# Weight low parts in two half-width GpSimd instructions, and the gated product rounded by ScalarE in the first two blocks

## The reference, cut to what matters

```python
def swiglu(x, w_gate, w_up, w_down):
    return (jax.nn.silu(x @ w_gate) * (x @ w_up)) @ w_down

x = x + 0.5 * swiglu(rms_norm(x, ffn1_norm[l]), ffn1_w_gate[l], ffn1_w_up[l], ffn1_w_down[l])
...      # mixer: indexer-selected sparse attention and multiscale pooling, w_in, w_out
x = x + 0.5 * swiglu(rms_norm(x, ffn2_norm[l]), ffn2_w_gate[l], ffn2_w_up[l], ffn2_w_down[l])
```

## Time and profile before

| | |
|---|---|
| median of 3 runs | 1928.82 us (1926.11 to 1929.69) |
| profiled execution | 1931.76 us, of it span 1930.0 us |
| mean granted TensorE clock | 0.961 |
| PE, PE weight load | 1820.7 us (94%), 1507.3 us (78%) |
| DVE, ACT, POOL | 1132.9 us (59%), 620.0 us (32%), 754.8 us (39%) |

### The profile page before, as it was taken

The page is one execution under the profiler, slowest core; times in us unless marked ns, Lnnn a source line. Parts: engine busy times, 40 slices in busy tenths (PEclk is TensorE's granted clock), DMA queues, the critical chain, the costliest instruction groups (busy, mean ns, idle before and its releaser), DMA issues. The chain is left out here.

```text
span 1930.0 us, 25162 instructions
## 1 busy us (share of the span) xinstructions
PE 1820.7 (94%) x8729; PEld 1507.3 (78%) x8729; DVE 1132.9 (59%) x1648; ACT 620.0 (32%) x1033; POOL 754.8 (39%) x370
## 2 busy tenths in 40 slices
PE   7999999999979999999999999899998699999995
PEld 6887778787756788788887888799887487887874
DVE  4525865867994368354145166565578764364467
ACT  4222112143455332122123133655512442232322
POOL 3543433447660235444444445100033144444434
PEclk9999999999989899999999999999999699999997
DMA  6435543533210245433323333100022133333211
GB/s 200 121 94 156 155 145 89 162 110 93 82 39 22 88 123 182 142 99 96 116 79 105 89 98 98 34 1 2 1 77 77 33 98 113 95 98 98 86 56 44
DMA packets 279689, 178.34 MB, mean 92 GB/s; under 512 B 6264, under 2 KB 258356, under 8 KB 279476
## 3 DMA queue, kind: packets, MB, share of 16 engines
q1 hardware_dynamic: 265348, 149.35, 26.7%
q10 hardware_dynamic: 14256, 27.87, 4.4%
HBM read 175.11 MB, written 2.10 MB: 92 GB/s over the span
## 5 line engine op out<-in xcount | busy, mean ns | idle before, releaser
L604 POOL TENSOR_TENSOR wL<-raw,wH 128x1024 fp32r<-128x1024 f32 (+2 forms) x280 | 681.6, 2440 | 1129.5 <-ACT wH L1126 1128.5
L672 PE MATMUL ps<-actH,wH 128*128 128x512 f32 x1280 | 507.6, 397 | 9.1 <-DVE actL L1878 5.6
L672 PE MATMUL ps<-actL,wH 128*128 128x512 f32 x1280 | 504.0, 394 | 0.0
L672 PE MATMUL ps<-actH,wL 128*128 128x512 f32 x1280 | 503.8, 394 | 0.0
L1126 ACT ACTIVATE wH<-raw 128x1024 fp32r<-128x1024 f32 (+2 forms) x280 | 285.8, 1029 | 452.3 <-PE ps L672 430.6
L672 PEld LDWEIGHTS ps<-actH,wH 128*128 128x128 f32 x1280 | 243.7, 190 | 64.8 <-issue 8.3
L672 PEld LDWEIGHTS ps<-actH,wL 128*128 128x128 f32 x1280 | 243.9, 191 | 51.9
L672 PEld LDWEIGHTS ps<-actL,wH 128*128 128x128 f32 x1280 | 244.1, 191 | 50.1
L672 PE MATMUL ps<-hidH,wH 128*128 128x512 f32 x656 | 261.0, 398 | 17.0 <-DVE hidL L1479 7.8
L672 PE MATMUL ps<-hidL,wH 128*128 128x512 f32 x656 | 259.4, 395 | 0.0
L672 PE MATMUL ps<-hidH,wL 128*128 128x512 f32 x656 | 259.1, 395 | 0.0
(11 more groups left out here) (293 smaller groups left out, 2267.4 us busy)
## 6 DMA issues: line engine op xcount, KB each, us to landing
mod_raw<-in_w_mod ACTq DMA_DIRECT2D x24, 1024.0 KB, 5.1
raw<-in_w_in SPq DMA_DIRECT2D x48, 512.0 KB, 3.7
raw<-in_ffn_w_gate SPq DMA_DIRECT2D x44, 512.0 KB, 3.9
raw<-in_ffn_w_up SPq DMA_DIRECT2D x44, 512.0 KB, 3.8
raw<-in_w_up SPq DMA_DIRECT2D x44, 512.0 KB, 3.8
raw<-in_ffn_w_down SPq DMA_DIRECT2D x32, 512.0 KB, 3.8
raw<-in_w_out SPq DMA_DIRECT2D x16, 512.0 KB, 3.9
raw<-in_w_down SPq DMA_DIRECT2D x16, 512.0 KB, 3.9
```

The lines of the kernel that those rows point to most:

```text
L604: nc.gpsimd.tensor_tensor(wL[:, a:a + w], raw[:, a:a + w], wH[:, a:a + w].bitcast(F32), ALU.subtract).then_inc(lo_ready, 1)
L672: return nc.tensor.matmul(out, a, b, start=first, stop=last)
```

## The change

Two edits. In `lows` the one subtraction of a slab becomes two of half the width, one behind the other, each of which raises `lo_ready`; everything that counts `lo_ready` counts twice as far, so that PE and SP still wait for both halves. In `hidden` DVE no longer rounds `h`: ACT does, in `drain` at odd j, ahead of the split of that slab, on a semaphore `h_ready`, and DVE waits for `h_high` before `hidL`. The counts of links in the loops fall by those that are gone. The feed-forward of the second block and the merge keep their own rounding on DVE.

```diff
         def slab(st, i, j, first=False):
             if not first:
-                sp.wait_ge(lo_ready, i * 4 + (st["base"] + j - 3))
+                sp.wait_ge(lo_ready, (i * 4 + (st["base"] + j - 3)) * 2)
...
                 pool.wait_ge(hi_ready, i * 4 + (st["base"] + j + 1))
-                nc.gpsimd.tensor_tensor(wL[:, a:a + w], raw[:, a:a + w], wH[:, a:a + w].bitcast(F32),
-                                        ALU.subtract).then_inc(lo_ready, 1)
+                for b in (a, a + w // 2):
+                    nc.gpsimd.tensor_tensor(wL[:, b:b + w // 2], raw[:, b:b + w // 2], wH[:, b:b + w // 2].bitcast(F32),
+                                            ALU.subtract).then_inc(lo_ready, 1)
...
                 for j in range(SLOTS):
-                    pe.wait_ge(lo_ready, i * 4 + (st["base"] + j + 1))
+                    pe.wait_ge(lo_ready, (i * 4 + (st["base"] + j + 1)) * 2)
...
                 if j % 2 == 0:
                     act.wait_ge(drained_v, i * 4 + (drain_base[name] + j + 1))
                     nc.scalar.activation(sg[:], g1[:], ACT.Silu).then_inc(silu_ready, 1)
+                else:
+                    f = i * 2 + j // 2
+                    act.wait_ge(h_ready, f + (SILU_BEFORE[name] + 1))
+                    nc.scalar.activation(tile(hidH, f), h[:], ACT.Copy).then_inc(h_high, 1)
...
             dve.wait_ge(silu_ready, f + (SILU_BEFORE[name] + 1))
-            link(V.tensor_tensor(h[:], sg[:], ur[:], ALU.mult))
-            link(V.tensor_scalar(tile(hidH, f), h[:], 1.0, None, ALU.mult))
+            V.tensor_tensor(h[:], sg[:], ur[:], ALU.mult).then_inc(h_ready, 1)
+            dve.wait_ge(h_high, f + (SILU_BEFORE[name] + 1))
             V.tensor_tensor(tile(hidL, f), h[:], tile(hidH, f).bitcast(F32), ALU.subtract).then_inc(hid_ready, 1)
```

More of the change, by code:

```diff
@@ L364, in _build @@
     silu_ready = sem("silu_ready")
+    h_ready, h_high = sem("h_ready"), sem("h_high")
     silu_c_ready = sem("silu_c_ready")
@@ L645, in _ @@
                     pool.wait_ge(q2_rot, 1)
-                    pool.wait_ge(lo_ready, st["base"])
+                    pool.wait_ge(lo_ready, (st["base"]) * 2)
                     for low, half in ((kLA, upper), (kLB, lower)):
@@ L733, in token_tiles @@
             for j in range(SLOTS):
-                pe.wait_ge(lo_ready, st["base"] + j + 1)
+                pe.wait_ge(lo_ready, (st["base"] + j + 1) * 2)
                 for kk in range(2):
@@ L771, in first_slabs @@
                 if k0 == 0:
-                    pe.wait_ge(lo_ready, j + 1)
+                    pe.wait_ge(lo_ready, (j + 1) * 2)
                 for k in range(k0, k1):
@@ L1044, in merge @@
             for j in range(SLOTS):
-                pe.wait_ge(lo_ready, i * 4 + (stage_of["merge"]["base"] + j + 1))
+                pe.wait_ge(lo_ready, (i * 4 + (stage_of["merge"]["base"] + j + 1)) * 2)
                 pe.wait_ge(drained_v, i * 4 + (drain_base["merge"] + j - 3))
@@ L1538, in modded_part @@
             modded(name, n, 0, hid0)
-            chain.loop(1, nf // 2, 2 * ((7 if ctx_too else 3) + 2) + (1 if ctx_too else 0),
+            chain.loop(1, nf // 2, 2 * (7 if ctx_too else 3) + (1 if ctx_too else 0),
                        lambda i: modded(name, n, i, hid0))
@@ L1550, in _ @@
             else:
-                chain.loop(0, nf // 2, 4, lambda i, f0=f0: [hidden("f1_up0", i, q, f0) for q in range(2)])
+                chain.loop(0, nf // 2, 0, lambda i, f0=f0: [hidden("f1_up0", i, q, f0) for q in range(2)])
             if n < 2:
@@ L1737, in _ @@
                             link(V.tensor_scalar(modc[:, 32:40], modc[:, 32:40], 1.0, None, ALU.add))
-                chain.loop(2 if n == 1 else 0, nf // 2, 4,
+                chain.loop(2 if n == 1 else 0, nf // 2, 0,
                            lambda i, n=n, f0=f0: [hidden(f"f2_up{n}", i, q, NF + KT + f0) for q in range(2)])
```

## The result

The changed kernel takes **1908.7 us** (median of 4 runs, 1906.35 to 1912.16); the kernel before took 1927.46 in its runs beside it (1925.87 to 1929.69). The ratio is 0.9903, with a 95% interval of 0.9883 to 0.9923. That is 18.8 us faster. The sign was right, the size was not, and 1911 had been the price of a rival that was given 0.12. One experiment further on (`e11`) has runs at two levels, 45 us apart, and is told with both; one run of `e3` (1940) stands apart from its other three in the same way.

The account below looks back on a forecast made before the run. It took PE, in flight for 94% of the span, to bound the kernel, so only its waits and clock cost time. Terms -1.4+2.1-3.0-2.15+0.4-1.6-0.5 = -6.15 us led to a median of 1922.7, range 1913 to 1931.

Parts of the forecast that it names:

- the size of a hold: DVE beside POOL's low parts: an operation meeting a half waits at most 1.29 us instead of 2.4.
- +0.6 per iteration: Stages where DVE multiplies for the modulation: each iteration grows by 0.6 us, blocked time passing to the products.
- `f1_up1` and `f2_up0`: First and second block's modulated up stages: +2.1 us (-1 to +4) and -2.15 us (-3.8 to +1).
- `f1_up2`'s end: Change to the down stage: wait of 2.12 us becomes 0.3 to 1.0, without clock loss: -3.0 us.
- The rounding on ACT: Ends of f1_up0, f2_up1 and f2_up2: hidL done 3.1 us after the slab, waits of 0.3 and 1.00 removed: -1.4 us.
- the new wait in `f1_down1`: PE waits there for the last modulation products, 2.9 us, and pays the clock again, 1.7.
- Clock: PE at half clock behind waits of some 2.1 us: 1.7 us of work lost each.
- Third block: Its three waits for hidL: no gain, 0 us, since chains of two or more blocked operations gain nothing.
- L1901 at 1.3 and L1902 above 1: Third block on DVE: h falls from 2.25 us on average to 1.3, the operation behind it rises from 0.43 to above 1.
- The slower one: Modulation stages decide: a half costs DVE 0.4 us more than allowed, an iteration grows by 1.6: 1933 us, chance 0.13.
- No change: Halves act as one, the second being already queued: about -3 us, 1926, chance 0.2.
- The 1911 rival: Every blocked operation gains; third-block waits fall by 1.2 each and lose clock loss, f1_up1 shortens: 1911 us, chance 0.12.

Follow-up runs that it names:

- e11: The changed kernel with each low part in eight subtractions, four in stage out1 beside the selection: 1877.26 us in three runs, 1922.63 in its other four.
- e3: The changed kernel with each slab's low part in four subtractions of a quarter width, ACT still rounding: 1896.53 us.
- e10_up1_full: The changed kernel with full-width low parts in stage f1_up1 alone, halves elsewhere: 1911.21 us.
- e2_act: The kernel before with only the rounding of h moved to ACT, low parts at full width: 1917.86 us.
- e6_third_full: The changed kernel with full-width low parts in the third block's stages, halves elsewhere: 1907.89 us.
- e4_eighths: The changed kernel with each low part in eight subtractions of an eighth of the width: 1925.87 us.
- e9_stall: The changed kernel with 4.2 us of extra DVE work ahead of the selection's last comparison, before the first attention: 1952.65 us.

## Why the prediction was wrong

- **The step that failed is the size of a hold**: "each half then stops one operation" was right, "waits at most 1.29" was a bound that I used as the size. The trace of before had the answer. The rows that I read don't decide it: `hidL` in the earlier trace rows starts 0.44 us behind POOL, so that 2.0 of standing still is what a whole record of 2.4 would give as well. The modulation products do, with DVE's queue full (ns, least, median, largest):

```profile
L1453 DVE SCALAR_TENSOR_TENSOR mod_acc<-mod_raw,silu_c,mod_acc x112: 750/752/2769, 171.5 to 855.9; 128x512 f32<-128x512 f32 x112
```

The longest is held 2.02, against a record of 2.40 where nothing is in the way: 0.4 of the record holds nothing. Take 0.4 from 1.29, and two halves cost 1.8 against 2.0, where I had 2.58 against 2.4. With that, +0.6 per iteration of the modulated stages becomes a gain: `f1_up1` measures 0.9 shorter an iteration, and by `e10_up1_full` and `e2_act` 0.7 of that are the halves. The two stretches that rested on this term, `f1_up1` and `f2_up0`, missed by 5.4 and 2.3 us; how much of that is this term alone, and how much the clock and the waits behind it, the runs don't split. The Trainium skill ("SBUF — State Buffer", Who interferes with whom) has the engines exclude each other for the whole instruction. I wrote that the trace agrees; it doesn't: 2.40, 1.29, 0.73 and 0.45 us of record hold 2.03, 0.91, 0.36 and 0.08.
- **`f1_up2`'s end**: -3.0 was too little by a microsecond. The wait went whole, since the copy on ACT pushes the split and the low part behind `hidL`. The move had been priced as a cost that is hidden, and its other side, POOL starting later, was not carried on.
- **The rounding on ACT** went as told: no wait at `f1_up0`, `f2_up1`, `f2_up2` (0.3 and 1.00 make 1.3, not 1.4), and 5.0 us on top of halves. So did the new wait in `f1_down1`, at 1.2 instead of 2.9.
- **Clock.** PE runs the same 8729 matmuls in both; its busy time fell by 8.8 us (1820.7 to 1811.9) and its idle time by 13.3 (109.3 to 96.0), so about 9 of the 22 us of the profiled pair are clock and 13 are waits. Span times (1 - clock) fell by more, from 75.3 to 61.1 us, because it also counts half speed while PE stands idle. I had charged the clock at three waits only. It also came back in places whose wait had not changed: behind the wait for `qB` ahead of the second attention, 4.3 in both, PE worked 4.5 us at half clock before and 3.4 after. Some of that is the execution: the profiled one of before lies 4.3 above its median of 1927.46, that of after 1.0 above its own, which is the difference between 22 and 18.8.
- **Third block**: zero is what `e6_third_full` can't tell from the truth, but its reason was wrong, so that it held is luck: the waits fell by 0.3 each, as two holds of 0.8 are less than the 1.8 in sum of `h` and `hidL` before. L1901 at 1.3 and L1902 above 1 came as told (L1907 and L1908 of after).
- **The rivals.** The slower one rested on a half costing more than its record and is refuted. "No change" supposed that the halves act as one; the two held operations at 1597.90 say no. The 1911 rival came nearest in time by the wrong road: it let the third block give 8.7 us.

## What to carry to other kernels

Read the hold of one engine on another from the operation that is held (its time less its clear time), never from the record of the holder, and at two widths if the trace has them. A long GpSimd elementwise instruction beside a busy VectorE is worth trying in four pieces, as here, but where VectorE's chain ends just ahead of a stage that doesn't bring the clock back, check that no operation is caught by back-to-back pieces. Look in the trace for such a stage: here a wait of 4.9 us ahead of one cost ten times the 4.2 us of work that made it, and filling the gap with four products of constants kept the clock.

## What the runs showed of the hardware

- A GpSimd subtraction of 1024, 512, 256 and 128 columns holds a VectorE product by 2.03, 0.91, 0.36 and 0.08 us, against records of 2.40, 1.29, 0.73 (`e3_quarters`, from 556.51) and 0.45 (`e4_eighths`, from 547.67) where nothing holds the subtraction. The difference is 0.37 to 0.38 at each width, so of an eighth nearly all holds nothing. Whether it is a part of GpSimd's instruction or of VectorE's that the other runs beside, the records don't tell. This was the surprise, and it is most of the gain.
- Taking turns can fail: one VectorE comparison of 0.43 us took 4.94 beside 17 eighths that ran back to back from 550.56 to 557.61, one operation of two inputs took 2.72 for 0.43 in the same trace, and in `e11_eighths_but_out1` two products `h` took 3.06 and 2.25 for 0.69. All four began inside a run of pieces of which each starts before the last has ended. So did a `hidL` at 191.74 in `e4_eighths`, and one piece alone held it: 0.99 us for 0.69. What sets the two cases apart isn't known. "Issue order, not op shape, decides who blocks", says the Trainium skill ("SBUF — State Buffer", Who interferes with whom); the eleven pieces that started after 552.95 still went ahead of the comparison, so the order of the starts does not explain it.
- The granted clock stayed at 0.50 for 99, 106 and 96 us in the first attention (`e4_eighths`, `e9_stall`, `e11_eighths_but_out1`), with PE in flight for 97.05 of the 98.99 us in the first of them. In the kernel before it stayed at 1.00 from the first product of the attention at 579.96 to 628.04. The fall came behind the wait: in `e11_eighths_but_out1` the attention began at 554.28 at 1.00 and ran at 0.50 from 555.81. Behind the waits for `mod_acc` and `hidL` in the stages of weight products of the profiled pair it was at 0.50 for 3.4 or 6.8 us, or not at all.
